# A two-block transformer in float32 on one core: both ends of the kernel in parts, transposes and VectorE chains at the norms moved, and the last head group of both attentions in product banks of its own

## The reference

```python
# layer 0 (A): indexer, top-64 keys per query, grouped softmax attention, gated
h = mixer_a(x, w_in_a, w_o_a, positions)      # (o * silu(gate)) @ w_o
x = layer_norm(ALPHA * x + h, ln_g[0], ln_b[0])
x = x + (p[0] @ w_ple[0]) * sigmoid(x @ w_ple_gate[0])
# layer 1 (B): stick-breaking attention, 16 heads in 4 groups, gated
h = mixer_b(x, w_in_b, w_o_b, k_sh, v_sh)     # (o * silu(gate)) @ w_o
x = layer_norm(ALPHA * x + h, ln_g[1], ln_b[1])
x = x + (p[1] @ w_ple[1]) * sigmoid(x @ w_ple_gate[1])
# second block (C): latent attention beside a bidirectional HGRN2, then the MLP
h = rmsnorm(x, pre_mix_g) * (1.0 + scale_a) + shift_a
mix = concatenate([attn_out, rec_out]) @ w_out
x = x + gate_a * rmsnorm(mix, post_mix_g)
h = rmsnorm(x, pre_mlp_g) * (1.0 + scale_m) + shift_m
y = square(relu(h @ w_up)) @ w_down
x = x + gate_m * rmsnorm(y, post_mlp_g)       # the output
```

## Time and profile before

| what | value |
|---|---|
| time, median of three runs (lowest to highest) | 2254.88 us (2252.53 to 2256.1) |
| the profiled execution's own time | 2255.14 us |
| its span, first to last instruction | 2253.3 us |
| mean granted TensorE clock | 0.992 |
| TensorE busy | 2184.6 us, 97% |
| VectorE busy | 1443.0 us, 64% |
| ScalarE busy | 1011.3 us, 45% |
| moved by DMA | 499.36 MB, mean 222 GB/s |

### The profile page before, as it was taken

The page is one execution under the profiler, slowest core; times in us unless marked ns, Lnnn a source line. Parts: engine busy times, 40 slices in busy tenths (PEclk is TensorE's granted clock), DMA queues, the critical chain, the costliest instruction groups (busy, mean ns, idle before and its releaser), DMA issues.

```text
span 2253.3 us, 24575 instructions
## 1 busy us (share of the span) xinstructions
PE 2184.6 (97%) x10387; PEld 1812.8 (80%) x10387; DVE 1443.0 (64%) x1415; ACT 1011.3 (45%) x995; POOL 3.9 (0%) x17
## 2 busy tenths in 40 slices
PE   8999989999999999999999999988999999999997
PEld 8878878777888787767888988867888888888886
DVE  5778656865766757767876775487545545545555
ACT  5443663434336633334454466544434433443441
POOL 0000000000000000000000000000000000000000
PEclk9999999999999999999999999999999999999999
DMA  8867638575976457758852325365656656655752
GB/s 288 309 235 283 231 138 343 207 293 178 344 287 240 167 189 301 262 221 315 334 207 92 131 85 197 115 239 200 211 187 231 226 188 213 244 187 189 260 188 110
DMA packets 73246, 499.36 MB, mean 222 GB/s; under 512 B 8881, under 2 KB 9393, under 8 KB 16305
## 3 DMA queue, kind: packets, MB, share of 16 engines
q1 hardware_dynamic: 72720, 497.66, 61.3%
q10 hardware_dynamic: 416, 0.13, 0.0%
HBM read 493.52 MB, written 4.24 MB: 221 GB/s over the span
## 4 chain that ended last, share of the span: by engine, by line
PE 89%; DVE 5%; ACT 2%; DMA 2%; issue 1%; ACTq 0%; DVEq 0%; SPq 0%
PE products L2283 65%; PE products L2294 13%; PE aside L2582 1%; DVE w_low L1377 1%; DMA raw<-in_w_c_f 1%; PE transposed L2700 1%; ACT w_high L795 1%; PE transposed L2357 1%; PE transposed L2401 1%; PE transposed L2429 1%; PE aside L2429 1%; DVE raw L1391 1%; DMA raw<-in_w_mod 0%; PE aside L2687 0%; PE products L2687 0%
## 5 line engine op out<-in xcount | busy, mean ns | idle before, releaser
L1377 DVE TENSOR_TENSOR w_low<-raw,w_high 128x2048 fp32r<-128x2048 f32 (+3 forms) x360 | 798.4, 2220 | 622.7 <-ACT w_high L795 622.3
L795 ACT ACTIVATE w_high<-raw 128x2048 fp32r<-128x2048 f32 (+3 forms) x360 | 668.8, 1859 | 904.9 <-PE products L2283 778.1
L2283 PE MATMUL products<-w_high,x_high 128*128 128x512 f32 (+2 forms) x1856 | 716.8, 386 | 14.9 <-DVE w_low L1377 11.0
L2283 PE MATMUL products<-w_high,x_low 128*128 128x512 f32 (+2 forms) x1856 | 709.2, 382 | 0.0
L2283 PE MATMUL products<-w_low,x_high 128*128 128x512 f32 (+2 forms) x1856 | 708.8, 382 | 0.0
L2283 PEld LDWEIGHTS products<-w_high,x_high 128*128 128x128 f32 x1856 | 349.6, 188 | 82.7 <-issue 14.7
L2283 PEld LDWEIGHTS products<-w_high,x_low 128*128 128x128 f32 x1856 | 349.6, 188 | 66.6
L2283 PEld LDWEIGHTS products<-w_low,x_high 128*128 128x128 f32 x1856 | 349.8, 188 | 66.3 <-issue 1.7
L1391 DVE SCALAR_TENSOR_TENSOR raw<-raw,cond_row 128x2048 f32<-128x2048 f32 x96 | 219.3, 2284 | 0.0
L2294 PE MATMUL products<-w_high,x_high 128*128 128x512 f32 (+1 forms) x496 | 203.9, 411 | 10.6 <-DVE w_low L1377 6.2
L2283 PE MATMUL products<-w_high,u_high 128*128 128x512 f32 x512 | 199.9, 391 | 0.0
(11 more groups left out here) (398 smaller groups left out, 1472.0 us busy)
## 6 DMA issues: line engine op xcount, KB each, us to landing
raw<-in_w_mlp SPq DMA_DIRECT2D x128, 1024.0 KB, 4.9
raw<-in_w_mod SPq DMA_DIRECT2D x96, 1024.0 KB, 5.0
raw<-in_w_ple SPq DMA_DIRECT2D x32, 1024.0 KB, 6.9
raw<-in_w_a_qkv SPq DMA_DIRECT2D x24, 1024.0 KB, 5.6
raw<-in_w_b_kvq SPq DMA_DIRECT2D x24, 1024.0 KB, 7.0
raw<-in_w_a_gate SPq DMA_DIRECT2D x16, 1024.0 KB, 5.8
raw<-in_w_a_out SPq DMA_DIRECT2D x16, 1024.0 KB, 6.8
raw<-in_w_b_gate SPq DMA_DIRECT2D x16, 1024.0 KB, 5.7
```

Of the source, the lines that this page charges most:

```text
L795: act.activation(m.hi[:, slot(st, u, j), 0:n], m.raw[:, RAW_SLOT[at], 0:n], ACT.Copy).then_inc(m.s_w_high, 1)
L1377: dve.tensor_tensor(m.lo[:, r, 0:n], m.raw[:, RAW_SLOT[at], 0:n], m.hi[:, r, 0:n].bitcast(F32), ALU.subtract).then_inc(m.s_raw_used, 1)
L2283: ins = pe.matmul(bank, x[:, x0 + kk, a], wt[(slice(None),) + w], start=first and kk == 0 and n == 0, stop=last and kk == st.kq - 1 and n ...
```

## The change

1. **Start in halves.** The first quarter of x and of the weights is loaded, split and multiplied in two halves, with two semaphores of their own.
2. **Attention tails.** Group 3 of both attentions uses `g[2:4]`, the second product pair, in place of `t`, and no longer waits for the split of group 1.
3. **Transposes.** The transposes of the third piece stand behind 9 matmuls of the second half instead of 3. This holds for all four norms by rows.
4. **Norm between mixer and MLP.** On VectorE w_low of quarter 0 moves behind the first normalised piece, x_low of the first piece ahead of the second piece, and x_low of the third piece to the place behind row 1's reciprocal. On ScalarE w_high of quarter 2 moves ahead of the third piece's x_high. TensorE waits for product pair 0 only at the first piece of row block 1.
5. **End in rows.** The last MLP unit is done row by row, and the whole chain behind it runs for row block 0 and then for row block 1, with eight stores of 256 KB instead of four of 512 KB.

```diff
-    m.pairs = [m.u, m.t]
+    m.pairs = [m.u, m.t, m.u, m.g[:, 2:4, :]]
...
-    for j in range(4):
+    h = 2 * a_idx.width
+    bring(m.x0t[:, 0:2, :], d.x_t[:, 0:2, :], m.s_first_x)
+    bring(m.raw[:, RAW_SLOT[0], 0:h], d.w["a_idx"][0, 0][:, 0:h], m.s_first_w)
+    bring(m.x0t[:, 2:4, :], d.x_t[:, 2:4, :], m.s_xt_landed[0])
+    bring(m.raw[:, RAW_SLOT[0], h:2 * h], d.w["a_idx"][0, 0][:, h:2 * h], m.s_landed[RAW_SLOT[0]])
+    for j in range(1, 4):
         bring(m.x0t[:, 4 * j:4 * j + 4, :], d.x_t[:, 4 * j:4 * j + 4, :], m.s_xt_landed[j])
         load_quarter(a_idx, 0, j, d.w["a_idx"][0, j])
...
-    for c in range(4):
-        sp.wait_ge(m.s_mlp_done, RB * c + RB)
-        bring(out.rearrange(tokens, p=P)[:, :, 512 * c:512 * c + 512], m.res[:, :, 512 * c:512 * c + 512], m.s_out_stored)
-    sp.wait_ge(m.s_out_stored, 64)
+    for rb in range(RB):
+        for c in range(4):
+            sp.wait_ge(m.s_mlp_done, 4 * rb + c + 1)
+            bring(out.rearrange(tokens, p=P)[:, rb, 512 * c:512 * c + 512], m.res[:, rb, 512 * c:512 * c + 512], m.s_out_stored)
+    sp.wait_ge(m.s_out_stored, 16 * 4 * RB)
...
-    std()
+    for rb in range(RB):
+        std(rb, rb + 1)
...
         inverse_std(rb, rb + 1)
+        if between:
+            between()
         for c in range(4):
             x = m.res[:, rb, chunk(c)]
             stt(x, m.mix[:, rb, chunk(c)], m.rstd[:, rb:rb + 1], x, ALU.mult, ALU.add).then_inc(m.s_x_added, 1)
...
     whole(0)
-    low_unit("mlp", 0, [0])
     add_row(6, 1)
     second(0)
     dve.wait_ge(m.s_rows2_landed, 48)
     mlp_normed(0, 0)
+    low_unit("mlp", 0, [0])
+    row_low(ROWS_THREE, 0)
     mlp_normed(0, 1)
-    row_low(ROWS_THREE, 0)
     low_unit("mlp", 0, [1])
     row_low(ROWS_THREE, 1)
     mlp_normed(0, 2)
     add_row(7, 1)
-    row_low(ROWS_THREE, 2)
-    whole(1)
+    whole(1, lambda: row_low(ROWS_THREE, 2))
...
-    lane.sync()
-    spread(4)
-    mean_square()
-    gain_chunk(3)
-    inverse_std()
-    for c in range(4):
-        for rb in range(RB):
+    for rb in range(RB):
+        y = m.y[:, rb, chunk(3)]
+        if rb == 0:
+            dve.wait_ge(m.s_first_rows, 4)
+        else:
+            dve.wait_ge(m.s_w_used, 4 * (mlp.g0 + mlp.units) + 4)
+        lane.link(dve.tensor_tensor(y, y, m.g[:, 2 + rb, :], ALU.add))
+        lane.link(dve.bn_stats(m.st[:, rb, 3, :], y))
+        lane.link(dve.bn_aggr(m.mv[:, rb, :], m.st[:, rb, 0:4, :]))
+        row_mean_square(rb)
+        lane.did(dve.tensor_tensor(y, y, m.z_pg[:, chunk(3)], ALU.mult))
+        inverse_std(rb, rb + 1)
+        for c in range(4):
             x = m.res[:, rb, chunk(c)]
             stt(x, m.y[:, rb, chunk(c)], m.rstd[:, rb:rb + 1], x, ALU.mult, ALU.add).then_inc(m.s_mlp_done, 1)
...
-            pe.wait_ge(m.s_g_free[0], st.s0 // 2 + 1)
+            if not kept_rows:
+                pe.wait_ge(m.s_g_free[0], st.s0 // 2 + 1)
             for i, (rb, c) in enumerate(items):
+                if kept_rows and (rb, c) == (1, 0):
+                    pe.wait_ge(m.s_g_free[0], st.s0 // 2 + 1)
...
-                ins = half(st, 0, c, m.g[:, rb], rb, 4 * c, c == 0, c == 3, (lambda: turn(i + 1)) if i + 1 < len(items) else None, 1 if i < 2 else 2)
+                ins = half(st, 0, c, m.g[:, rb], rb, 4 * c, c == 0, c == 3, (lambda: turn(i + 1)) if i + 1 < len(items) else None, (1, 3)[i] if i < 2 else 2)
...
-        if c >= 2:
-
-            pe.wait_ge(split, c - 1)
-        banks = m.pairs[c % 2]
+        if c == 2:
+
+            pe.wait_ge(split, 1)
+        banks = m.pairs[c]
...
+            elif last and k == 7:
+                row_by_row(None)(mlp, 8 * q + k, mlp.s0 // 2 + 4 * q + k // 2, k % 2, None, *xs)
```

More of the change, by code:

```diff
@@ L893, in row_high @@
             lane.n["T"] += 1
-    for c in range(4):
+    h = 2 * PLAN["a_idx"].width
+    act.wait_ge(m.s_first_x, 16)
+    act.activation(m.xh[:, 0:2, :], m.x0t[:, 0:2, :], ACT.Copy).then_inc(m.s_first_x, 1)
+    act.wait_ge(m.s_first_w, 16)
+    act.wait_ge(m.s_w_used, 5 - RING)
+    act.activation(m.hi[:, 0, 0:h], m.raw[:, RAW_SLOT[0], 0:h], ACT.Copy).then_inc(m.s_first_w, 1)
+    act.wait_ge(m.s_xt_landed[0], 16)
+    act.activation(m.xh[:, 2:4, :], m.x0t[:, 2:4, :], ACT.Copy).then_inc(m.s_x_high_ready, 1)
+    act.wait_ge(m.s_landed[RAW_SLOT[0]], 16)
+    act.activation(m.hi[:, 0, h:2 * h], m.raw[:, RAW_SLOT[0], h:2 * h], ACT.Copy).then_inc(m.s_w_high, 1)
+    for c in range(1, 4):
         act.wait_ge(m.s_xt_landed[c], 16)
@@ L1549, in vector_program @@
     dve.memset(m.grow[:], 1.0).then_inc(m.s_gain_ones, 1)
-    for c in range(4):
+    h = 2 * PLAN["a_idx"].width
+    dve.wait_ge(m.s_first_x, 17)
+    dve.tensor_tensor(m.xl[:, 0:2, :], m.x0t[:, 0:2, :], m.xh[:, 0:2, :].bitcast(F32), ALU.subtract).then_inc(m.s_first_x, 1)
+    dve.wait_ge(m.s_first_w, 17)
+    dve.tensor_tensor(m.lo[:, 0, 0:h], m.raw[:, RAW_SLOT[0], 0:h], m.hi[:, 0, 0:h].bitcast(F32), ALU.subtract).then_inc(m.s_first_w, 1)
+    dve.wait_ge(m.s_x_high_ready, 1)
+    dve.tensor_tensor(m.xl[:, 2:4, :], m.x0t[:, 2:4, :], m.xh[:, 2:4, :].bitcast(F32), ALU.subtract).then_inc(m.s_x_low_ready, 1)
+    lane.n["xh"] += 1
+    dve.wait_ge(m.s_w_high, 1)
+    dve.tensor_tensor(m.lo[:, 0, h:2 * h], m.raw[:, RAW_SLOT[0], h:2 * h], m.hi[:, 0, h:2 * h].bitcast(F32), ALU.subtract).then_inc(m.s_raw_used, 1)
+    for c in range(1, 4):
         k = slice(4 * c, 4 * c + 4)
@@ L2146, in mix_gain_row, with whole @@
         lane.did(dve.tensor_tensor(x, x, m.x_pg[:, chunk(c)], ALU.mult))
-    def whole(rb):
+    def whole(rb, between=None):
         lane.sync()
@@ L2270, in tensor_program, with quarter @@
     lane = Lane(pe, m.s_pe_step)
-    def quarter(st, u, j, pair, x0, first, last, xh=m.xh, xl=m.xl, middle=None):
-        pe.wait_ge(m.s_raw_used, quarter_at(st, u, j) + 5)
+    def quarter(st, u, j, pair, x0, first, last, xh=m.xh, xl=m.xl, middle=None, whole=True):
+        if whole:
+            pe.wait_ge(m.s_raw_used, quarter_at(st, u, j) + 5)
         for kk in range(st.kq):
+            if not whole and kk == st.kq // 2:
+                pe.wait_ge(m.s_raw_used, quarter_at(st, u, j) + 5)
             if middle and kk == st.kq // 2:
@@ L2285, in quarter, with half @@
         ins.then_inc(m.s_w_used, 1)
-    def half(st, u, j, bank, rb, x0, first, last, middle=None, at=1):
+    def half(st, u, j, bank, rb, x0, first, last, middle=None, at=1, xh=m.xh, xl=m.xl):
         for kk in range(st.kq):
@@ L2306, in row_by_row, with last @@
     def row_by_row(begin):
-        def last(st, u, half_s, pair, aside):
+        def last(st, u, half_s, pair, aside, xh=m.xh, xl=m.xl):
             pe.wait_ge(m.s_g_free[pair], half_s + 1)
             for j in range(2):
-                quarter(st, u, j, pair, 4 * j, j == 0, False)
+                quarter(st, u, j, pair, 4 * j, j == 0, False, xh, xl)
             for j in range(2, 4):
                 pe.wait_ge(m.s_raw_used, quarter_at(st, u, j) + 5)
-                ins = half(st, u, j, m.g[:, 2 * pair], 0, 4 * j, False, j == 3)
+                ins = half(st, u, j, m.g[:, 2 * pair], 0, 4 * j, False, j == 3, xh=xh, xl=xl)
                 if aside:
@@ L2435, in first_columns @@
         pe.wait_ge(m.s_g_free[0], st.s0 // 2 + 1)
+        pe.wait_ge(m.s_first_x, 18)
+        pe.wait_ge(m.s_first_w, 18)
         for j in range(4):
-            pe.wait_ge(m.s_x_low_ready, j + 1)
-            quarter(st, 0, j, 0, 4 * j, j == 0, j == 3)
+            if j:
+                pe.wait_ge(m.s_x_low_ready, j + 1)
+            quarter(st, 0, j, 0, 4 * j, j == 0, j == 3, middle=None if j else (lambda: pe.wait_ge(m.s_x_low_ready, 1)), whole=j > 0)
     gemm("a_idx", None, first_columns)
@@ L2906, in tensor_program @@
     mlp = PLAN["mlp"]
-    _, first = rows_arriving(m.mix, ROWS_THREE)
+    _, first = rows_arriving(m.mix, ROWS_THREE, True)
     t0 = lane.n["T"] + 8
```

23 lines of the change are left out of this document (13 added, 10 removed).

## The result

The changed kernel took 2246.34 us (median of five runs, 2244.89 to 2246.94), against 2256.1 for the kernel before on the same chip (2252.53 to 2259.23): ratio 0.9953, 95% interval 0.9942 to 0.9964. By the medians it is 9.8 us faster, by the interval of the ratio 8.1 to 13.1 us. It lies in the range given (2241.0 to 2247.5), 2.9 us above the forecast.

What follows compares the result with a forecast made beforehand. TensorE, busy for 97% of the span, was taken as the bound, so only its gaps and both ends could be won. Gains of 0.5 + 2.67 + 0 + 1.25 + 1.9 + 5.2 = 11.5 us off 2254.88 gave 2243.4, range 2241.0 to 2247.5.

Steps and rivals of the forecast that it cites:

- Start: Kernel start: TensorE begins earlier, but quarter 4's weight load and split bound it, so only -0.5 us, ends 0 and -0.8.
- Attention A: Tail of the first attention: the last group's 2.67 us wait for x_low of group 1 goes, -2.67 us.
- Attention B: Tail of the second attention: TensorE's wait is for ScalarE's exponentials, which stay, so 0 us, ends 0 and -0.1.
- Three norms: Norms behind both attentions and before c_f: later transposes of the third piece fill waits, -1.25 us in all.
- Mixer norm: Norm between mixer and MLP: all 1.91 us of VectorE's idle goes, -1.9 us, ends -1.1 and -2.1.
- End: Behind the last product: row 0's chain runs early and the smaller stores overlap, -5.2 us, ends -4.4 and -5.8.
- The second: Rival, whole kernel: low clock falls elsewhere, +2 to +5 us, total -8, 2246.9 us; chance 0.12.
- The third: Rival, c_f stretch: its chain with a 10.35 us load swallows gains won above, total -7.1, 2247.8 us; chance 0.07.
- The first: Rival, kernel start: the earlier start pays in full, -2.4 us, total -13.4, 2241.4 us; chance 0.08.
- the fourth: Rival, kernel end: stores don't overlap, end term +0.7 instead of -5.2, total -5.6, 2249.3 us; chance 0.03.
- the fifth: Rival, first attention's tail: the wait is only renamed, as in the second attention, total -8.8, 2246.1 us; chance 0.02.
- The sixth: Rival, from the gap before quarter 4 on: added low clock makes it slower (30 us: +3.6, 2258.5 us); chance 0.02.

## Why the prediction came out as it did

**Start: wrong, and its sign too.** The failed step is "from 10 to 22 us the DMA engines are full, with the same bytes in the same order as after the change, so this landing does not move". The rate there is indeed full, but the bytes ahead of it arrived late: with four loads of half size the engines moved 308 GB/s over 3 to 8 us, with whole ones 386. Quarter 4's load landed 0.8 us later and its w_high began 1.3 us later. The bound itself was right: with whole loads, TensorE starts 1.07 us earlier and has 0.28 or less of it at 24 us, and only moving quarter 4 frees more. Term: +1.2 for -0.5.

**Attention A:** -2.89 for -2.67; no wait took its place. The 0.2 is mostly what a bracket leaves out: it counts from the end of the product before, and products overlap. In the rows one lasts 0.39 us and the next starts after 0.23, so 0.16 us of lost pace stand ahead of the bracket. **Attention B:** 0, for the reason given: the wait is for ScalarE's exponentials, and putting them first brings 2.8. The gain of 1.64 that the trace shows there is a spell that did not come.

**Three norms:** -0.38, -0.35 and -0.32 make -1.05 for -1.25. In the first and the second norm the two waits were 0.76 and 0.72 for 0.7 and 0.95 foreseen, so the chain from normalised piece to x_low sets the end, as worked out.

**Mixer norm:** VectorE -2.03 for -1.91; TensorE -2.27. The closest margin I named, the square root for row 1 (1518.7 against 1518.8), was real: in the changed kernel VectorE has no idle there, with the start undone it has 0.60. The low clock of this norm lasted 10 us in that trace and 7 in the changed kernel's, which fits the prediction's remark on a longer one, but no run isolates it.

```profile
1515.26 0.16 DVE L1489 RECIPROCAL rstd<-rstd 128x1 f32<-128x1 f32 x1 [0.60 <-ACT rstd L886]
```

**End:** -5.2 for -5.2. The stores overlap, so the Trainium skill's rule (DMA: Bandwidth & Descriptors, section on measured bandwidth) to batch to 1 MiB does not decide here: what counts is when the last bytes may go, and 512 KB was 0.5 us worse. At the start the same rule points the right way, though both sizes lie below 1 MiB: loads of 512 KB gave 386 GB/s, of 256 KB 308.

**Rivals.** The second came nearest: spells moved, +1.61 at the start and +1.58 at 531, and one less in B (-1.64), net +1.55 in this trace. The third did not happen: what was won above c_f was not lost in it, and a wait there shrank. The first fell with quarter 4, the fourth with the rate of 382, the fifth with attention A alone. The sixth, more low clock, did not come: the mean clock is 0.993 for 0.992.

**The sum.** Own terms in this trace: +1.20, -2.89, 0, -1.05, -2.27, -5.2 are -10.2, for -11.5 foreseen. The start falls short by 1.7 and the three norms by 0.2, and A and the mixer norm bring 0.6 more. Spells (+1.55) and the wait at 1115 (-1.39) were in no term. That they nearly cancel is luck: either alone is nearly as large as the largest error of a term. By the timed runs the change gave 9.8, which leaves 1.7 of the 2.9 us above the forecast; the other 1.2 is that before, too, came out higher beside it (2256.1 for 2254.88).

## What to carry to other kernels

Halving the first loads to start an engine sooner delayed whatever queued behind them here. Splitting only the work on the data cost nothing, but little of the earlier start was left at the fifth quarter, so first ask which load the engine needs next: moving that one forward is what kept 0.66 us and more. Where two results release an engine at about the same time, taking one away brings nothing; look who is queued ahead of the other one. Judge changes of one or two microseconds by the trace, instruction by instruction, since one spell of lower clock is as large.
